# Hybrid mixer block: earlier decay sums and exponentials in the linear attention, gate slices last in a softmax step

## What is computed

```
def body(state, inp):                       # gla_chunk_scan, one direction
    cum = jnp.cumsum(lai, axis=2)           # lai: log decays
    last = cum[:, :, -1:, :]
    new_state = exp(last)*state + einsum('bhsd,bhse->bhde', ki * jnp.exp(last - cum), vi)
    o_inter = jnp.einsum('bhtd,bhde->bhte', qi * jnp.exp(cum), state)
    decay = jnp.exp(jnp.where(lower_tri, cum_t - cum_s, -jnp.inf))
    scores = jnp.einsum('bhtd,bhsd,bhtsd->bhts', qi, ki, decay)
    return new_state, o_inter + jnp.einsum('bhts,bhse->bhte', scores, vi)
...
y = from_heads(rmsnorm(o_f + flip(o_b), norm_w)) * jax.nn.silu(gate)   # readout
...
z = jnp.einsum('blnw,nwd->blnd', jnp.stack(ys, axis=2), w_branch)      # gated_merge
return jnp.einsum('blnd,blnd->bld', jax.nn.sigmoid(gate_logits), z) @ w_o
```

## Time and profile before

| | |
|---|---|
| median of 3 runs | 3343.31 us (3334.99 to 3349.95) |
| profiled execution | 3357.3 us, its span 3355.6 us |
| TensorE busy | 3134.9 us, 93% of the span |
| VectorE, ScalarE busy | 42%, 35% |
| TensorE's mean granted clock | 0.964 of full |

### The profile page before, as it was taken

The page is one execution under the profiler, slowest core; times in us unless marked ns, Lnnn a source line. Parts: engine busy times, 40 slices in busy tenths (PEclk is TensorE's granted clock), DMA queues, the critical chain, the costliest instruction groups (busy, mean ns, idle before and its releaser), DMA issues.

```text
span 3355.6 us, 39886 instructions
## 1 busy us (share of the span) xinstructions
PE 3134.9 (93%) x16256; PEld 2418.2 (72%) x16256; DVE 1414.6 (42%) x2288; ACT 1167.2 (35%) x2019; POOL 165.6 (5%) x179
## 2 busy tenths in 40 slices
PE   6988899999999999899999989888999999889998
PEld 4877785577667768788888867777456567578887
DVE  4266742333443435423232332774333444454444
ACT  4343333333443343412121234443332443442222
POOL 0023300000000000000000000320000000000000
PEclk8999998999999999999999989999997999999999
DMA  5222240031103123233333322223021021323332
GB/s 186 75 84 79 81 135 25 19 106 62 52 27 113 59 92 102 78 105 101 101 106 102 95 82 60 85 76 126 7 80 47 13 89 48 107 76 100 94 99 90
DMA packets 83759, 273.82 MB, mean 82 GB/s; under 512 B 9344, under 2 KB 9600, under 8 KB 82688
## 3 DMA queue, kind: packets, MB, share of 16 engines
q1 hardware_dynamic: 74896, 229.84, 21.7%
q0 software_dynamic: 8688, 41.49, 3.7%
HBM read 245.07 MB, written 26.21 MB: 81 GB/s over the span
## 4 chain that ended last, share of the span: by engine, by line
PE 87%; ACT 5%; DVE 5%; issue 2%; DMA 2%; SPq 0%; DVEq 0%; ACTq 0%
PE slot L615 84%; PE slot L1019 2%; DMA raw<-w_merge_dram 1%; ACT tmp L1209 1%; DVE wl L1517 1%; ACT PT_B L1392 0%; ACT Hh L1211 0%; DMA SS<-g_kept 0%; ACT wh L1118 0%; DVE XS L1783 0%; ACT Yh L1386 0%; ACT logits_out L1161 0%; DVE XS L1722 0%; DMA X<-xT_dram 0%; DMA g_kept<-logits_out 0%
## 5 line engine op out<-in xcount | busy, mean ns | idle before, releaser
L615 PE MATMUL slot<-Hh,wh 128*128 128x512 f32 (+1 forms) x2368 | 885.9, 375 | 48.4 <-DVE Hl L1564 15.1
L615 PE MATMUL slot<-Hl,wh 128*128 128x512 f32 (+1 forms) x2368 | 843.2, 357 | 0.0
L615 PE MATMUL slot<-Hh,wl 128*128 128x512 f32 (+1 forms) x2368 | 841.9, 357 | 0.0
L615 PEld LDWEIGHTS slot<-Hh,wh 128*128 128x128 f32 x2368 | 455.4, 193 | 166.4 <-issue 77.7
L615 PEld LDWEIGHTS slot<-Hh,wl 128*128 128x128 f32 x2368 | 455.2, 193 | 64.9
L615 PEld LDWEIGHTS slot<-Hl,wh 128*128 128x128 f32 x2368 | 456.3, 193 | 61.1 <-issue 5.8
L1517 DVE TENSOR_TENSOR wl<-raw,wh 128x1024 fp32r<-128x1024 f32 (+1 forms) x208 | 228.5, 1099 | 232.5 <-ACT wh L1118 229.5
L1841 DVE TENSOR_REDUCE rowmax<-slot 128x1 f32<-128x768 f32 (+3 forms) x160 | 123.4, 771 | 412.6 <-PE slot L615 412.0
L615 PE MATMUL slot<-Uh,wh 128*128 128x512 f32 (+1 forms) x768 | 274.3, 357 | 0.0
L615 PE MATMUL slot<-Ul,wh 128*128 128x512 f32 (+1 forms) x768 | 272.0, 354 | 0.0
L615 PE MATMUL slot<-Uh,wl 128*128 128x512 f32 (+1 forms) x768 | 271.5, 354 | 0.0
(11 more groups left out here) (229 smaller groups left out, 4099.8 us busy)
## 6 DMA issues: line engine op xcount, KB each, us to landing
raw<-w_dram SPq DMA_DIRECT2D x204, 512.0 KB, 3.6
raw<-w_gate_dram SPq DMA_DIRECT2D x64, 512.0 KB, 3.6
ada_g_raw<-ada_dram POOLq DMA_DIRECT2D x48, 512.0 KB, 3.9
ada_g_raw<-ada_dram SPq DMA_DIRECT2D x32, 512.0 KB, 3.9
raw<-w_merge_dram SPq DMA_DIRECT2D x64, 256.0 KB, 2.7
g_kept<-logits_out SPq DMA_DIRECT2D x32, 384.0 KB, 2.3
SS<-g_kept SPq DMA_DIRECT2D x32, 384.0 KB, 3.3
ada_first<-ada_dram SPq DMA_DIRECT2D x8, 1024.0 KB, 18.2
```

Source lines behind the costliest of these rows:

```text
L615: return pe.matmul(dst, lhsT, rhs, start=start, stop=stop)
```

## The change

In branch C, TensorE makes `decay_logits(h + 1)` ahead of level product 6 and no longer ahead of product 7. VectorE runs `decay_sums` of the next head ahead of the last overlay, and no longer after it. It makes the decayed keys ahead of the decayed queries, then the readout; `output_low` comes after the first query products, and the `wl` of the whole gate jobs all at level 1. ScalarE makes the five exponentials ahead of the norm factors, and the exponentials of level 0 ahead of the copies of whole gate jobs. Product 0 waits for the first whole gate's copy alone, and product 1 for all of them. In layer 1 a slice comes behind its level product and no longer ahead of it. In a softmax step the slice comes last, behind values and transposes. No arithmetic is added or removed.

```diff
@@ -875,7 +875,7 @@
 
 
                     for n in range(len(LEVELS) + 1):
-                        if n == len(LEVELS) and h + 1 < C_HEADS:
+                        if n == len(LEVELS) - 1 and h + 1 < C_HEADS:
                             decay_logits(h + 1)
                         where = n % 2
                         if n == 1:
@@ -884,11 +884,8 @@
                             buffer = level_buffer(max(n - 1, 0))
                             left, right = ks[buffer], qs[buffer]
                         more = steps[h * (len(LEVELS) + 1) + n]
-                        if nq == SEQ:
-                            for step in more:
-                                later_gate(layer, level_gate(layer, h, step[0]), *step[1:])
-                        if n == 0:
-                            pe.wait_ge(logits_copied.sem, parts_done[0])
+                        if n < 2:
+                            pe.wait_ge(logits_copied.sem, parts_done[0] - (WHOLE_GATES[layer] - 1 if n == 0 else 0))
                         pe.wait_ge(*slots.next(("level", where), acc_first if n == 0 else lvl_read))
                         if n != 1:
                             pe.wait_ge(k_ready.sem, w.next(k_ready))
@@ -904,6 +901,9 @@
                                 s, d = slice(c * P, (c + 1) * P), slice((c - LB) * P, (c - LB + 1) * P)
                                 last = mm(level_ctx_at[where][:, d], left[:, s], right[:, s])
                         last.then_inc(lvl_done.sem, 1)
+                        if nq == SEQ:
+                            for step in more:
+                                later_gate(layer, level_gate(layer, h, step[0]), *step[1:])
                         if n == 0:
 
                             pe.wait_ge(*slots.next("c1", state_ready))
@@ -988,8 +988,6 @@
                                 else:
                                     last = mm(out_s[:, lo:hi], QY[:, h, qs_], KD[:, h // (D_HEADS // D_KV), lo:hi])
                         last.then_inc(scores_done.sem, 1)
-                        for step in steps[i]:
-                            later_gate(layer, FIRST_GATE[layer][branch] + step[0], *step[1:])
                     if i > LAG and tiles[i - LAG - 1]["last"]:
 
                         tile = tiles[i - LAG - 1]
@@ -1020,6 +1018,9 @@
                             last.then_inc(prob_t.sem, 1)
                             units += 1
                             values_in += 1
+                    if i < len(tiles):
+                        for step in steps[i]:
+                            later_gate(layer, FIRST_GATE[layer][branch] + step[0], *step[1:])
                 chain_over(("c0", "c1", ("unit", 0), ("unit", 1), "values"))
 
             def merge(branch, layer, nq, groups):
@@ -1305,17 +1306,13 @@
 
                 def levels_over():
 
-                    act.wait_ge(lvl_done.sem, w.next(lvl_done, len(LEVELS)))
                     act.wait_ge(q_ready.sem, w.next(q_ready, 2))
                     act.wait_ge(k_ready.sem, w.next(k_ready, 2))
 
                 for h in range(C_HEADS):
                     if h > 0:
-                        norm_factors()
                         levels_over()
 
-                    for i in range(WHOLE_GATES[layer] - 1):
-                        whole_out(layer, i, True)
                     act.wait_ge(diff_ready.sem, w.next(diff_ready))
                     act.activation(ee[0][f, 0:T], cumy[f, 0:T], ACT.Exp, scale=1.0 / C_TEMP)
                     act.activation(ee[0][b, 0:T], diff[0][b, 0:T], ACT.Exp, scale=1.0 / C_TEMP)
@@ -1323,8 +1320,8 @@
                     act.activation(ee[1][b, 0:T], cumy[b, 0:T], ACT.Exp, scale=1.0 / C_TEMP)
                     act.activation(dec[:, :], tot[:, :], ACT.Exp, scale=1.0 / C_TEMP).then_inc(inter_e.sem, 1)
                     if h > 0:
-                        output_high(h - 1)
-                    whole_out(layer, WHOLE_GATES[layer] - 1, True)
+                        norm_factors()
+                        act.wait_ge(lvl_done.sem, w.next(lvl_done, len(LEVELS)))
                     for n, m in enumerate(LEVELS):
                         if n == 0:
 
@@ -1340,8 +1337,13 @@
                         act.activation(e[:, :, 0:m], d[:, :, 0:m], ACT.Exp, scale=-1.0 / C_TEMP)
                         act.activation(e[:, :, m:2 * m], d[:, :, m:2 * m], ACT.Exp, scale=1.0 / C_TEMP).then_inc(e_ready.sem, 1)
                         if n == 0:
+                            if h > 0:
+                                output_high(h - 1)
+                            whole_out(layer, 0, True)
                             act.wait_ge(kt_done.sem, w.next(kt_done))
                             act.activation(kit, slot[0][:, 0:T], ACT.Copy).then_inc(kt_copied.sem, 1)
+                            for i in range(1, WHOLE_GATES[layer]):
+                                whole_out(layer, i, True)
                         if n == 1:
                             act.wait_ge(lvl_done.sem, w.next(lvl_done))
                             ins = act.activation(acc[:, 0:SEQ], level_at[0], ACT.Copy)
@@ -1699,7 +1702,6 @@
 
                 def readout(h):
 
-                    dve.wait_ge(oc_done.sem, w.next(oc_done))
                     dve.wait_ge(rstd_ready.sem, w.next(rstd_ready))
                     dve.tensor_tensor(kit[:, 0:nq], slot[1][:, 0:nq], kit[:, 0:nq], ALU.mult).then_inc(oc_read.sem, 1)
                     dve.wait_ge(oc_read.sem, w.next(oc_read))
@@ -1712,8 +1714,6 @@
                     dve.tensor_tensor(Yl[:, h, 0:nq], QY[:, h, 0:nq], Yh[:, h, 0:nq].bitcast(f32), ALU.subtract).then_inc(y_low.sem, 1)
 
                 for h in range(C_HEADS):
-                    if h > 0:
-                        decay_sums(layer, h)
 
                     def difference(n):
                         m = LEVELS[n]
@@ -1740,15 +1740,13 @@
 
                     gates_low(h, -1)
                     difference(0)
+                    dve.wait_ge(inter_e.sem, w.next(inter_e))
+                    dve.tensor_tensor(ki, kk[:, h, :], ee[1], ALU.mult)
+                    if h > 0:
+                        dve.wait_ge(oc_done.sem, w.next(oc_done))
+                    dve.tensor_tensor(qi[:, 0:nq], qq[:, h, 0:nq], ee[0][:, 0:nq], ALU.mult).then_inc(inter_qk.sem, 1)
                     if h > 0:
                         readout(h - 1)
-                    dve.wait_ge(inter_e.sem, w.next(inter_e))
-                    dve.tensor_tensor(qi[:, 0:nq], qq[:, h, 0:nq], ee[0][:, 0:nq], ALU.mult)
-                    dve.tensor_tensor(ki, kk[:, h, :], ee[1], ALU.mult).then_inc(inter_qk.sem, 1)
-                    if h > 0:
-                        output_low(h - 1)
-                    for i in range(WHOLE_GATES[layer] - 1):
-                        whole_out()
                     ds = slot[1][:, 0:T].rearrange("p (b s) -> p b s", s=P)
                     orders = ((f, [LB + c for c in range(NB - LB)] + list(range(LB))),
                               (b, [NB - 1 - c for c in range(NB)]))
@@ -1766,7 +1764,8 @@
 
                     for n, m in enumerate(LEVELS):
                         if n == 1:
-                            whole_out()
+                            for i in range(WHOLE_GATES[layer]):
+                                whole_out()
                         if n >= 3:
                             gates_low(h, n - 3)
                         if n >= 2:
@@ -1781,6 +1780,8 @@
                         s3 = qq[:, h, 0:nq].rearrange("p (b s) -> p b s", s=2 * m)
                         dve.tensor_tensor(q3[f, :, m:2 * m], s3[f, :, m:2 * m], e3[f, :, m:2 * m], ALU.mult)
                         dve.tensor_tensor(q3[b, :, 0:m], s3[b, :, 0:m], e3[b, :, 0:m], ALU.mult).then_inc(q_ready.sem, 1)
+                        if n == 0 and h > 0:
+                            output_low(h - 1)
                         if n == 1:
                             dve.wait_ge(lvl_done.sem, w.next(lvl_done))
                             gates_out(h, 0)
@@ -1797,11 +1798,14 @@
                     gates_out(h, hooks - 2)
                     overlay(len(LEVELS) - 1)
                     gates_low(h, hooks - 3)
+                    if h + 1 < C_HEADS:
+                        decay_sums(layer, h + 1)
                     gates_out(h, hooks - 1)
                     overlay(len(LEVELS))
                     gates_low(h, hooks - 2)
                     dve.wait_ge(lvl_read.sem, w.next(lvl_read))
                 gates_low(C_HEADS, -1)
+                dve.wait_ge(oc_done.sem, w.next(oc_done))
                 readout(C_HEADS - 1)
                 output_low(C_HEADS - 1)
                 for i in range(WHOLE_GATES[layer]):
```

## The result

| | before | changed |
|---|---|---|
| median, device us | 3335.88 (10 runs, 3326.41 to 3355.04) | 3309.13 (10 runs, 3297.56 to 3319.99) |
| ratio | | 0.9914, 95% interval 0.9888 to 0.9940 |
| profiled execution, span | 3357.3, 3355.6 | 3308.35, 3306.6 |
| mean granted clock of the profiled one | 0.964 | 0.976 |

A forecast was written before the change was run, and what follows sets the result against it. TensorE was taken as the bound, with only idle gaps and clock to win. Branch C's layer 0 -7.7, layer 1 -0.8 and softmax 0 gave -8.5 us, from 3343.3 to 3335 us; 80% range 3313 to 3354.

The forecast's parts named there:

- Boundary of heads in layer 0: Branch C, heads 1 to 3: earlier product 0 against later output, net -0.6 us at each of three boundaries.
- Output to output in layer 1: Branch C: a head takes 52.3 us against 50.78 with the sums in VectorE's chain, 1.5 us more, twice.
- Last head: Branch C, layer 1: with no decay sums to make, it takes 46.3 us against 50.5, -4.2 us.
- The 2.84 us wait at hook 5: Branch C, layer 1, wait for a copy of logits: about 1 us won, shrinking to about 1.8 us.
- I put the losses at 5.5 us and the sum at 0: Softmax branches: removed waits against later transposes cancel to 0, with -5 and +8 us as ends.
- In D I expect nothing: Softmax branch D: no gain, since the chain from scores to copied probabilities gets no shorter with transposes first.
- short of 0.4 to 1.0 us: Softmax steps where ScalarE also rounds a weight: the banks come free that much too late, about eight times.
- they just meet: D of layer 1: in about half the steps the next transposes come just as the two banks are free, 3.0 us after scores.
- (a): Rival: clock stays up at the seven gaps' new places, about -20 us, 3323 us; chance 0.17.
- (b): Rival: long 1.2 GHz stretch in B of layer 1 spared, 3314 us (0.12), or one added in layer 0, 3356 (0.05).
- (c): Rival: transposes wait 0.4 us for banks in each of layer 1's 64 steps, +17 us, 3361 us; chance 0.14.
- (d): Rival: decay sums reach further, low clock costs 1.7 us more at six boundaries, +10 us, 3345 us; chance 0.12.

The follow-up runs named there:

- e2: The changed kernel with the old order in the softmax branches, so the edits of branch C alone: 3329.5 us, 0.9974 of the kernel before.
- e3: The changed kernel with the next head's decay sums back behind the last overlay: 3337.9 us, 0.9989 of the kernel before.
- e1: The kernel before with only the gate slice moved last in a softmax step, both layers: 3322.4 us, 0.9939 of the kernel before.
- e6: The kernel before with slices last in a softmax step in layer 0 only: 3325.5 us, 0.9964 of the kernel before.
- e12: The changed kernel, unedited, profiled once more: 31 us at half clock in the first 65 us of B in layer 1.

## Why the prediction was wrong

**Branch C was right in its mechanism, and close in most terms.** Product 0 on time in all heads: yes. Outputs 5 to 6 us idle with the clock at 0.50 behind: 5.38 and 4.93, and half clock in part of the time behind all of them. Boundary of heads in layer 0: forecast -0.6, measured -0.9 and -0.5. Output to output in layer 1: forecast 52.3, measured 51.8 and 51.6. Last head: 46.3 forecast, 46.4 measured. The 2.84 us wait at hook 5, the slice beside product 5, became one of 1.42 for that product's queries. Alone the half brings 8.4 us (e2), against 8.5; that these agree so closely is in part luck, since 3.8 of the 8.4 us are the clock's and known to 7 us only. That engines take their work in order, on which this rested, is what e3 shows: with the sums behind the overlay the output starts on time.

**The step that failed is that on the softmax branches, "I put the losses at 5.5 us and the sum at 0".** e1 measures -9.8 us at equal clock, and -19.6 with the clock. The 3.6 us of waits in B of layer 0 were in the forecast and are gone, as it said. Three other things in it were wrong.
- "In D I expect nothing": the four waits for logits in D of layer 0 (1.03 and three times 0.69 us) did go, because with the slice last a step lies between a job's end and the next one's start. Part came back ahead of the values (0.70, 0.70, 0.27 and 0.82, where one of 0.72 stood before). Net, D takes 105.2 us against 106.7 without a fall of the clock.
- The losses of 5.5 us were half of that. Waits for the transposed probabilities' copies went from 6.7 to 6.4 us ahead of the transposes (L1019, now L1017) and from 4.1 to 7.2 ahead of the values: 2.8 us. The mechanism exists. This is the step in D of layer 1 in which ScalarE rounds a weight first, and where "short of 0.4 to 1.0 us" was forecast:

```profile
2788.76 1.04 ACT L1119 ACTIVATE wh<-raw 128x1024 fp32r<-128x1024 f32 x1
2789.71 0.86 ACT L1395 ACTIVATE PT_B<-slot 128x384 f32<-128x384 f32 x2
...
2790.33 0.84 PE L1017 MATMUL slot<-ident,SS 128*128 128x128 f32 x6 [1.10 <-ACT PT_B L1395]
```

  Within the steps of layer 1 it came three times (0.43, 0.87 and 1.10 us), where the forecast had it about eight times and more; "they just meet" had been counted as a loss.
- That a step without waits gets 0.05 us shorter, and that a fall of the clock at a branch's end goes with a wait there, had no term.

**The clock had no term of the right size.** At equal clock the change is -13.6 us, which would have been inside the range. The other 16.7 us (give or take 5.5) are a mean clock of 0.9745 instead of 0.9692. Known places: branch C of layer 0, where the time lost to the clock (half of that spent at 1.2 GHz, idle time included) is 15.4 us in all three profiles of the kernel before, and 8.5 and 10.2 in the two of the changed one (the forecast had 2.4 of this), and the end of B of layer 0, some 3. The remaining 8 us aren't settled. In the same five profiles the largest further item is the long stretch in B of layer 1, 18.2 us on the mean against 7.7, and its scatter is larger than that difference.

**The rivals.** (a) fell: the clock does drop at the gaps' new places, six and not seven as it counted. (b) looked right from one profile of each kernel, and would have been the story: 21 us for a stretch that is gone. e6 and e12 show it absent with the old order and present with the new. The price of the stretch is real, its link to the change isn't shown. (c) fell: transposes wait no longer than before. (d) fell, since C gave what was forecast, and the wait ahead of the sum of squares in layer 0 is 0.90 us before and after.

**The base.** The profiled run and the three times given lay high: 86 runs of the kernel before have a median span of 3338.6 us, which is a time of 3340, some 3 us under the 3343 from which the forecast was taken. The ten beside the changed kernel have 3335.9, so of the 26 us between the forecast 3335 and the measured 3309, 7 are the base.

## What to carry to other kernels

Where runs scatter, compare kernels by a line of span against mean granted clock: it told 3 us apart in a scatter of 30, and it separates what an edit removes from what the clock gave. Don't credit an edit with a clock stretch that one profile has and another lacks; profile the old kernel again first. When a change moves two links of one chain together, try all four corners: here each edit needed the other, and leaving both out was the best.

## What the runs showed of the hardware

The mean granted clock of one and the same program varied from 0.964 to 0.974 between executions, 37 us of span, 1.1%; the residual beside the clock is 2.5 us. The Trainium skill calls the start-up cost of the clock variable from run to run and "<1% of a typical kernel span" (TensorE: Matmul & The Clock Gate, Part 1: The HAM clock gate); for the start the traces agree, since in the three profiles of the kernel before the first 100 us lose 6.8 to 8.5 us to the clock, 0.2 to 0.3% of the span. The scatter is larger than that, and stretches lie in the middle of the kernel too. One of them had TensorE busy throughout, as the row of the kernel before shows:

```profile
2553.00:2602.00 49.00, 49.00 (x126) 30.88 (x127) 15.26 (x39) 12.10 (x34) 0.00 (x0) 0.51 0.09 27
```

Rows without a gap, 49.00 us busy of 49.00, and still half the clock: a full engine in the profile doesn't mean that the clock comes back.
